# One decoder layer on one core: head pairs in prompt attention, another order of loads and of the MLP's steps, last product by token halves

## The reference

```
mods = silu(c) @ w_ada + b_ada                     # six vectors of 1024: shift, scale, gate, twice
h = rms_norm(x, norm_mix) * (1 + mods[1]) + mods[0]
q, k, v, u = split(h @ w_in, [512, 1024, 1536])    # w_in is 1024 x 2048
# prompt: causal softmax attention over blocks of 256 with a T5 bias (both blocks are in reach)
# samples: q . mean(k of each past block of 256), the top 3 of 16 blocks and the own tokens attend,
#          k and v come from pages of 128 rows through page_table
# pool:   trailing means of u over 2, 4, 8, 16, minus the token, times w_pool, times pool_scale
x = x + g1 * (concat(attn, pool) @ w_out)
h = rms_norm(x, norm_mlp) * (1 + sc2) + sh2
x = x + g2 * (square(relu(h @ w_up)) @ w_down)
y = rms_norm(x, norm_final)
```

## Time and profile before

| | |
|---|---|
| median of 3 runs | 983.2 us (982.89 to 991.43) |
| profiled execution | 986.67 us, its span 984.9 us |
| TensorE busy | 902.2 us, 92% |
| VectorE, ScalarE, GpSimd busy | 524.7, 231.2, 125.4 us |
| mean granted TensorE clock | 0.958 of 2.4 GHz |
| moved by DMA | 254.25 MB, 258 GB/s mean |

### The profile page before, as it was taken

How to read it: one execution, slowest core, us unless ns; L and a number is a source line. 1 busy time by engine, 2 the same in 40 slices (tenths; PEclk the granted TensorE clock), 3 DMA queues, 4 the chain that set the end, 5 groups by cost and what they waited for, 6 DMA issues and landing times.

```text
span 984.9 us, 16914 instructions
## 1 busy us (share of the span) xinstructions
PE 902.2 (92%) x6621; PEld 616.8 (63%) x6621; DVE 524.7 (53%) x968; ACT 231.2 (23%) x390; POOL 125.4 (13%) x134
## 2 busy tenths in 40 slices
PE   4699999999899887899899999899899799999896
PEld 3367775555676565666666666666666467675454
DVE  5533314787784766746756766667564232242224
ACT  3242204333220312220320320320220222213102
POOL 0006600000000000210210110110110111202100
PEclk8789999999999889899999999999999799999998
DMA  9902265888688586967977987887875957559992
GB/s 305 345 1 87 86 215 209 303 283 272 191 315 287 174 300 233 348 222 266 370 261 248 376 292 238 353 290 252 335 268 184 351 182 251 180 186 383 398 393 93
DMA packets 133282, 254.25 MB, mean 258 GB/s; under 512 B 10550, under 2 KB 61483, under 8 KB 125003
## 3 DMA queue, kind: packets, MB, share of 16 engines
q1 hardware_dynamic: 95571, 183.54, 53.0%
q10 hardware_dynamic: 36864, 67.13, 19.7%
q0 software_dynamic: 768, 2.51, 0.6%
HBM read 248.57 MB, written 4.75 MB: 257 GB/s over the span
## 4 chain that ended last, share of the span: by engine, by line
PE 70%; DVE 10%; DMA 8%; ACT 3%; issue 3%; ACTq 3%; SPq 1%; POOL 1%; DVEq 0%; POOLq 0%
PE PS L1523 68%; DVE KT L1120 4%; ACTq L849 3%; DMA VR<-in_cache_v_dram 2%; DMA VR<-in_w_up_dram 1%; DMA KR<-in_w_up_dram 1%; DMA KT<-in_w_up_dram 1%; ACT W_split L812 1%; PE PS L1692 1%; DMA W<-in_w_up_dram 1%; DMA X<-in_rel_bias_dram 1%; DMA KR<-in_cache_k_dram 1%; DVE smp L1239 1%; ACT smp L781 1%; PE PS L2098 0%
## 5 line engine op out<-in xcount | busy, mean ns | idle before, releaser
L1523 PE MATMUL PS<-H_split,W_split 128*128 128x512 f32 (+1 forms) x672 | 228.5, 401 | 2.0 <-DVE hT_split L1057 2.0
L1523 PE MATMUL PS<-gT_split,W_split 128*128 128x512 f32 x512 | 172.8, 402 | 3.0 <-POOL kT_split L681 3.0
L1120 DVE STREAM_TRANSPOSE KT<-KR 128x512 f32<-128x512 f32 x256 | 161.3, 680 | 18.7 <-DMA KR<-in_cache_k_dram 18.4
L1523 PEld LDWEIGHTS PS<-H_split,W_split 128*128 128x128 f32 x672 | 128.9, 195 | 50.0 <-issue 25.7
L1523 PE MATMUL PS<-hT_split,W_split 128*128 128x512 f32 (+1 forms) x336 | 131.5, 392 | 0.0
L1523 PEld LDWEIGHTS PS<-gT_split,W_split 128*128 128x128 f32 x512 | 96.1, 188 | 49.6 <-issue 18.7
L1270 DVE TENSOR_TENSOR W_split<-W,W_split 128x1024 fp32r<-128x1024 f32 x64 | 80.9, 1268 | 84.5 <-ACT W_split L812 84.5
L812 ACT ACTIVATE W_split<-W 128x1024 fp32r<-128x1024 f32 x64 | 67.2, 1052 | 230.1 <-DMA W<-in_w_up_dram 132.5
L1523 PE MATMUL PS<-KT,qcur 128*32 128x128 f32 (+1 forms) x2080 | 76.1, 289 | 29.0 <-DVE KT L1120 27.7
L1523 PE MATMUL PS<-kT_split,W_split 128*128 128x512 f32 x256 | 100.3, 392 | 0.0
L1309 DVE SCALAR_TENSOR_TENSOR xT<-PS,mods,xT 128x512 f32<-128x512 f32 x64 | 47.8, 749 | 80.6 <-PE PS L1523 80.6
(11 more groups left out here) (273 smaller groups left out, 963.2 us busy)
## 6 DMA issues: line engine op xcount, KB each, us to landing
KR<-in_cache_k_dram SPq DMA_DIRECT2D x256, 256.0 KB, 4.8
VR<-in_cache_v_dram ACTq DMA_DIRECT2D x256, 256.0 KB, 4.6
W<-in_w_up_dram SPq DMA_DIRECT2D x32, 512.0 KB, 6.7
W<-in_w_down_dram SPq DMA_DIRECT2D x32, 512.0 KB, 6.9
VR<-in_w_ada_dram SPq DMA_DIRECT2D x8, 1024.0 KB, 7.2
smp<-in_w_ada_dram SPq DMA_DIRECT2D x8, 1024.0 KB, 5.9
W<-in_w_in_dram SPq DMA_DIRECT2D x3, 2048.0 KB, 9.0
VR<-in_w_up_dram SPq DMA_DIRECT2D x3, 2048.0 KB, 10.6
```

Source lines behind the costliest of these rows:

```text
L1120: dve.transpose(ktb[:, t % 2, s, :], kring[:, t % 2, s, :]).then_inc(kt_ev, 1)
L1523: return pe.matmul(out, lhsT, rhs, start=start, stop=stop, **kw)
```

## The change

It is many edits at once; constants are `PAIRS = HP * TT` (16), `LAST = N_CH - 1`, `FINAL = (0, TT, 1, 2, 3)`, and TAIL_AT is gone. By place:

- Front: `load_ada(0)` is issued ahead of four small loads; TensorE's list goes modulation(0), state transposes, in_spread, modulation(1), (2), the bias matmuls (now in banks 6 and 0), modulation(3). VectorE evaluates the bias tables behind the last first_low. farb is negated, and the near bias gets it added at eviction (eight ScalarE copies of 256 columns for four of 512).
- Prompt attention goes by pairs of heads, q = (pair, tile).
- The half loads from j = 2 on are issued by ScalarE behind the eviction of pair j - 2.
- SyncE issues keys ahead of parts in every step; w_out for the samples in eight pieces, one a step at t = 66 to 73.
- The samples' output product is at t = 75, their MLP starts at t = 77; `sample_down(7)` is at 85.
- `values_ahead(t)` on ScalarE loads values t - LAG + 2, in step t behind some of its work; before, they were loaded first thing in step t + 1. TensorE weighs values ahead of `mlp(t, 0)` except at x == 3.
- VectorE turns keys ahead of weights_low at x == 1 and 3, and own_heads comes ahead of a weights_low at x == 2.
- `down` at x == 4 runs k = 0 to 2 of both tiles, then k = 3.
- The last chunk's down product goes by token halves, twice as many matmuls of 256 columns.

```diff
 # SyncE
+            for t in range(END + 1):          # first in the step, was behind the parts
+                if t + 2 < KT_ALL: ... load_keys(t + 2, k_ids)
+                if t == LAST_STEP:
+                    load_tail(0)
+                if t == LAST_STEP + 1:
+                    load_tail(1)
+                    load_tail(2)
+                if t >= LAST_STEP + 3:
+                    for n in (2 * (t - LAST_STEP - 3) + 2, 2 * (t - LAST_STEP - 3) + 3): ... load_tail(n)
...
-                    sp.dma_start(tail_slot(1), wout_d[:, :, 0:PIECE]).then_inc(tail_landed[1], 16)
-                    sp.wait_ge(qk, KT_ALL)
-                    sp.dma_start(tail_slot(2), wout_d[:, :, PIECE:D]).then_inc(tail_landed[2], 16)
+                if KT_ALL + 2 <= t < KT_ALL + 10:
+                    half, q = (t - KT_ALL - 2) // 4, (t - KT_ALL - 2) % 4
+                    sp.wait_ge(v_used, t - LAG)
+                    if half:
+                        sp.wait_ge(qk, KT_ALL)
+                    sp.dma_start(tail_slot(1 + half)[:, 2 * q:2 * q + 2, :],
+                                 wout_d[:, 2 * q:2 * q + 2, half * PIECE:(half + 1) * PIECE])\
+                      .then_inc(tail_landed[1 + half], 16)
 # ScalarE, attention
+            def exponentials(q):
+                n, s = (q % TT + 1) * P, 2 * (q % 2)
+                act.wait_ge(at_max, q + 1)
+                if q >= 2:
+                    act.wait_ge(at_pT, q - 1)
+                for e in range(2):
+                    act.activation(logits[:, s + e, 0:n], bank(e, P, n), ACT.Exp, bias=stat[:, s + e:s + e + 1],
+                                   accum_out=stat[:, 4 + s + e:5 + s + e]).then_inc(at_exp, 1)
+            def normalize(q):
+                act.wait_ge(at_rden, q + 1)
+                for e in range(2):
+                    act.activation(logits[:, s + e, 0:n], logits[:, s + e, 0:n], ACT.Copy,
+                                   scale=stat[:, 4 + s + e:5 + s + e]).then_inc(at_norm, 1)
+            for q in range(PAIRS):
+                if q + 1 < PAIRS:
+                    normalize(q + 1)
+                act.wait_ge(at_pT, q + 1)
+                if q:
+                    act.wait_ge(at_out, q)
+                for e in range(2):
+                    act.activation(pT[:, e, 0:n], bank(5 + e, P, n), ACT.Copy).then_inc(at_pT_ev, 1)
+                if q + 2 < PAIRS:
+                    act.wait_ge(ada_part, 4 + q + 1)
+                    act.dma_start(half_slot(q + 2), half_source(q + 2)).then_inc(half_landed[q % 2], 16)
+                if q + 2 < PAIRS:
+                    exponentials(q + 2)
+                if q > TT and q % TT == 1:
+                    attention_out(q // TT - 1)
 # ScalarE, MLP, x == 1 (x == 0, 5, 6, 7: values_ahead first; 2: behind relu; 3, 4: last)
                     relu(c, 0)
+                    values_ahead(t)
+                    hidden_high(c, 0)
                     if b < DB:
                         exps(b)
-                    hidden_high(c, 0)
                     weights_high(8 * c + 3 if c else 5)
 # VectorE, attention
+            def logits_in(q):
+                part = PS[:, 0:2, n - near:n]
+                link(dve.tensor_tensor(part, part, nearb[:, 2 * hp:2 * hp + 2, 2 * P - near:2 * P], ALU.add))
+                dve.tensor_reduce(stat[:, s:s + 2], PS[:, 0:2, 0:n], AX.X, ALU.max, negate=True).then_inc(at_max, 1)
+            def denominators(q):
+                dve.wait_ge(at_exp, 2 * q + 2)
+                dve.reciprocal(stat[:, 4 + s:6 + s], stat[:, 4 + s:6 + s]).then_inc(at_rden, 1)
+            for q in range(PAIRS):            # denominators(q+1), half_out(q), turn_keys, logits_in(q+2),
+                ...                           # half_modulation(q), turn_keys
 # VectorE, MLP, x == 1
+                    turn_unit(t + 1)
                     weights_low(8 * c + 3 if c else 5)
-                    turn_unit(t + 1)
 # TensorE, attention
+            def scores(q):
+                if q:
+                    pe.wait_ge(at_exp, 2 * q)
+                for e in range(2):
+                    r = slice(HD * e, HD * e + HD)
+                    last = mm(bank(e, P, (i + 1) * P), qT[r, hp, i * P:(i + 1) * P], kT[r, hp, 0:(i + 1) * P])
+                last.then_inc(at_scores, 1)
+            def weigh(q):
+                for kt in range(i + 1):
+                    for e in range(2):
+                        lo = HD * (2 * hp + e)
+                        last = mm(PS[HD * e:HD * e + HD, (4, 7)[hp % 2], i * P:(i + 1) * P], v_tok[:, kt, lo:lo + HD],
+                                  pT[:, e, kt * P:(kt + 1) * P], kt == 0, kt == i, skip_group_check=True)
+            for q in range(PAIRS):            # half_modulation(q), score_keys, scores(q+2), turn_prompt(q),
+                ...                           # weigh(q-1), fold_half(q)
 # TensorE, own values
-                    quarter(4, 0, probsT[0:NS, KEYS:], vS, False, True).then_inc(pv, 1)
+                    for q in range(QUADS):
+                        last = quarter(4, q, probsT[0:NS, KEYS:], vS[:, P * q:P * q + P], False, True, P, P * q)
 # TensorE, last chunk and end
+            def last_bank(j):
+                return bank((BANKS, (0, 1, 4, 7))[j // FT][j % 4], P, HALF, j // FT * HALF)
+                elif c == LAST and x == 4:
+                    for j in range(4):
+                        last_down(j, *((0, HP - 1), (HP - 1, HP))[half])
+                elif c == LAST:
+                    for j in range(2):
+                        last_down(4 * (x - 4) + 2 * half + j)
+                if t == END - 2:
+                    final_rows(0)             # between the halves; final_rows(1) behind the step
+                if t == END - 1:
+                    final_rows(2)             # between the halves; (3) and (4) behind the loop
```

More of the change, by code:

```diff
@@ L420, in softmax_of, with final_view, two @@
             return (t - 8) // 8
+        def final_view(p, n):
+            at = (2, 5)[p % 2]
+            return PS[0:n, at:at + 2, :]
+        def two(tile):
+            return tile.rearrange("p (a b) -> p a b", a=2)
+        def last_bank(j):
+            return bank((BANKS, (0, 1, 4, 7))[j // FT][j % 4], P, HALF, j // FT * HALF)
         @block.sync
@@ L1746, in _ @@
             scores(0)
-            scores(1)
             pe.wait_ge(bias_back, 16)
@@ L1972, in up, with down @@
                         ins.then_inc(up_ps, 1)
-            def down(c, m):
+            def down(c, m, first=0, end=HP):
                 if m >= 4:
                     pe.wait_ge(dn_ev, FT * c + m - 3)
-                for k in range(HP):
+                for k in range(first, end):
                     if m == 0:
```

605 lines of the change are left out of this document (309 added, 296 removed).

## The result

The changed kernel took 942.74 us (median of 4 runs, 940.84 to 947.47), the kernel before 984.3 us in the same set of runs; the ratio is 0.9564, 95% interval 0.9517 to 0.9610. Forecast were 936 us, range 922 to 954. The profiled execution took 941.84 us with a span of 940.0, against 984.9 before: 44.9 us less, where the sum said 47.7. One run of experiment 12 was in the chip's slower state and is left out of its median.

The account below looks back on a forecast made before the run. The prediction took TensorE, busy 92% with 70% of the chain, to bound the kernel, so only less TensorE work or fewer gaps could pay. Its eight terms summed to -47.7 us from 983.2, said as 936 us, range 922 to 954.

Parts of the forecast that it names:

- 1, front: Start to first projection product: bias matmuls fall where TensorE waits for DMA, projection begins at 48.4; -1.8 us.
- 2, attention: Prompt attention: a pair costs (4.1 + landing)/2, taken as 5.5 us, 93.7 in all; -2.3 us.
- rival (b): Prompt attention and own values: array parts don't overlap, 6.0 us a pair; 949 us in total, chance 0.09.
- (a): Prompt attention: half loads land late, 6.3 us a pair; 948 us in total, chance 0.17.
- 3, output stage: Output stage: keys issued ahead of parts end a late key unit, later parts cost nothing; -5.5 us.
- 4, chunks: MLP chunks 0 to 4: keys turned ahead of weight splits end TensorE's waits; chunk 0 -7.2 us, the others -14.2.
- 5, own values: Samples' own values: four parts of 128 columns run beside each other instead of 512-column matmuls; -5.3 us.
- 6, after the keys: Steps after the keys: w_out in pieces and earlier value loads end late values and half clock; -10.9 us.
- 7, tail: From 842.1 us to the end: stalls 4.5 us as before, end cut from 19.3 to 9; -5.5 us.
- 8, new waits: ScalarE's value loads wait for TensorE's weighing, and attention has half-clock spells; +5 us (0 to +15).
- (c): Seven chunks and stages: some 2.2 us of key wait returns in each as waiting for ScalarE; 951 us, chance 0.12.
- (d): Chunks with values: ScalarE's queue becomes the bound, 70 us over six chunks; 1006 us in total, chance 0.02.

Follow-up runs that it names:

- experiment 12: The changed kernel with three moves in its first half (bias products, add_sums at t = 16, value loads behind the same step's weighing): 959.09 us, ratio 0.9714.
- experiments 5 and 11: The changed kernel with w_out in two 2 MB loads (ratio 0.9604), and the changed kernel with the last down product by full width (945.3 us, ratio 0.9608).
- experiment 5: The changed kernel with w_out for the samples again as two 2 MB loads issued together: 942.4, 944.4, 953.3 and 954.2 us, ratio 0.9604.
- experiment 7: The changed kernel with the half loads of prompt attention issued by SyncE again: 943.88 us, ratio 0.9575.
- Experiment 6: The changed kernel with SyncE issuing keys behind the parts of the step again: 948.38 us, ratio 0.9614.
- experiment 1: The changed kernel with the samples' value weighing again between the two halves of the products in the MLP's steps: 966.45 us, ratio 0.9803.
- experiment 4: The changed kernel with the samples' own values again as one product of 512 columns: 948.64 us, ratio 0.9617.
- experiments 1 to 3: The changed kernel with one thing undone each: value weighing ahead of the products (966.45 us), VectorE's order at x == 1 and 3 (983.36), ScalarE's value-load place (954.22).
- Experiment 8: The changed kernel with half of the bytes of each load of the samples' MLP weights left out: 931.24 us, ratio 0.9460.

## Why the forecast held, point by point

**1, front: wrong, +1.5 for -1.8.** The step that failed: the bias matmuls would lie where TensorE waits for DMA. In the changed kernel:

```profile
33.55 1.92 PE L1580 MATMUL PS<-W,cT 128*32 128x512 f32 x16
37.76 1.69 PE L1580 MATMUL PS<-cst,sums 128*128 128x9 f32 x8 [2.29 <-DVE sums L1016]
39.38 4.94 PE L1580 MATMUL PS<-X 32*8 32x383 f32 x16
44.25 3.64 PE L1580 MATMUL PS<-KR,cT 128*32 128x512 f32 x16
```

TensorE is a chain of slow products and VectorE hand-overs by then, at 1.2 GHz in part; it reaches the fourth piece at 44.25 without a wait, 3.3 us after it did before. I had placed the work in a gap that belonged to the old order. It isn't the only step: in two of the traces (experiments 5 and 11) TensorE did come in time, at 41.7 and 41.9, and still began the projection at 50.0 and 50.2, since the product (3.64 us for the 2.8 forecast) and what follows ran at 1.2 GHz (granted clock 0.50 from 41.7 to 50.0 in experiment 5). In the twelve traces with this front the projection begins at 50.0 to 54.0, never near 48.4. (The terms of that sum give 48.2.)

**2, attention: right in size, its bound not shown: -6.3 for -2.3** (projection included; -4.7 without). Pairs 2 to 15 take 5.4 us each, 5.5 forecast. Of the 4.0 us beyond the forecast 2.4 lie in attention and are the chance of one trace: by the median of the other traces it is 2.9 us longer, 94.2 for the 93.7 forecast. Scores halved, where I took a quarter off: in the trace before, 512-column scores of two heads took 2.1 us, now 1.06. The weighing group of 16 products of 64 columns takes 1.02 us, 64 ns each for 128 before (the earlier trace rows has 8 of them in a group of 1.09); rival (b) is out. So is (a): its sign was there, gaps ahead of the half modulation in 6 of 16 pairs, at 0.65 us on average. The page of the Trainium skill that the forecast held against this move (Trainium Kernel Development and Optimization, Key Constraints: queues of SyncE and ScalarE share the 16 engines, only issue time is saved) agrees with the time of experiment 7 (943.9 for 942.7), and cuts both ways: the issuer is worth nothing that can be told in either direction. With it the forecast's formula for a pair, (4.1 + landing)/2, is in doubt: experiment 7 took the hand-over out of the 4.1, and a pair takes as long. TensorE waits for a load in six pairs only, all of slot VR.

**3, output stage: direction right, -1.7 for -5.5.** "The parts come later: nothing" was the step: the parts indeed cost nothing, the value pages did (2.4 us at 361, with slow clock behind it). The step of key unit 20 still takes 11.6 us, where the forecast had 8.2. Experiment 6 shows the exchange.

**4, chunks: the cause right, chunk 0 too high and the others too low.** Chunk 0 gave 3.6 of 7.9, since a wait of 2.8 for values (at 394, with a granted clock of 0.74 in that step) and one of 0.9 for smp fall into it. Chunks 1 to 3 gave 19.0 for 12.1: the waits for keys went as forecast, and a term is missing. The forecast named that TensorE weighs values ahead of the products and gave it no price. By experiment 1 it is 0.41 us in a plain step with keys. That is 1.2 us a chunk, or 1.6 if the third step, where the waits hide it, gains the same: 3.7 to 4.9 of the 6.9 us that chunks 1 to 3 gave beyond the forecast, and 6 to 8 in all. The rest stays open. A page of the Trainium skill states the rule that I left out (TensorEngine Tiling (Array Packing), Tiling Modes, Key Properties): a change of tiling mode, not merely of tile, drains TensorE. The traces fit it, with 0.2 us for each change between 32 and 128 columns.

**5, own values: right**, 0.35 us a group for 0.97, -5.0 of -5.3 (experiment 4).

**6, after the keys: right in sum.** From t = 56 to 75 it was -17.6; the forecast's terms give -16.9, and the joined order, which it did not count, pays in chunk 4 only (1.2 to 1.6), since without keys it saves no change. No value wait over 0.7 us is left. The pieces alone didn't remove it: with two big loads again the values were still in time (experiment 5).

**7, tail: wrong, +1.7 for -5.5.** The failed term is "stalls 4.5, as before". They were 12: 7.6 us around 857 (a wait of 4.40, then 1.2 GHz), 2.67 at 889, 1.09 at 906, and smaller ones. The two sides of it, VectorE and ScalarE:

```profile
855.54 1.22 DVE L1303 TENSOR_TENSOR W_split<-W,W_split 128x1024 fp32r<-128x1024 f32 x1 [10.58 <-ACT W_split L846]
856.68 0.68 DVE L1483 COPY scm<-PS 128x512 f32<-128x512 f32 x1
```
```profile
854.45 1.06 ACT L846 ACTIVATE W_split<-W 128x1024 fp32r<-128x1024 f32 x1 [10.48 <-DMA W<-in_w_up_dram]
```

Samples' weights and the last chunk's parts share a full DMA (share 1.05), a part lands at 854, and the sums' copy is queued behind its split. Three steps earlier, the samples' part shares its stretch with the parts; the 7.9 us of transfer against 4.7 of slack stood in my own sum, but I kept the old stalls instead of letting the difference show. The end, 9.6 us, was forecast at 9.0, though its terms as written add up to 9.65.

**8, new waits: not found.** ScalarE holds up no chunk: TensorE has 0.2 us of gaps in 64.8. Rivals (c) and (d) are out for the chunks; experiment 12 shows that (d)'s mechanism is real where ScalarE's own work stands behind such a load, in the output stage.

The total was right because errors cancelled. Chunks 1 to 3 gave 6.9 us more than forecast, the stretch behind them 0.7, attention with the projection 4.0, and 5.0 were charged for nothing: 16.6. Against them stand the front with 3.3, the output stage with 4.5, chunk 0 with 4.3 and the tail with 7.2: 19.3. That the total fell within 7 us owes something to luck. The parts aren't additive either: undone one by one, the three that are clear of noise (experiments 1 to 3) cost 76 us together, for 41.6 in all, since each was made with the others in place.

None of the versions that move all bytes is faster than the changed kernel. Experiment 8 says what the tail has to give, 11 us for 16 MB less. Moving them earlier needs slots that aren't free; that wasn't tried.

## What to carry to other kernels

Count the changes between products of different column widths in a step, and lay like beside like: two changes less gave 0.41 us of a 7.95 us step here, without a gap in the trace that would point there. When several queues are reordered together, price each order against the other engines' new places, not against the old trace; the dearest wait of the old order can grow (2.54 us to 4.61). Where a stretch has a DMA share of 1, moving a copy picked another wait, moving the issues cost 8.8 us, and only fewer bytes gave anything. And a stage of one trace is one sample: the same attention took 90.5 to 100.4 us.

## What was not expected of the hardware

A switch between 128x32 and 128x128 products costs 0.2 us without any gap showing in the trace (7.94 us with four against 7.54 with two, for equal work; 6.70 in both orders where both have two). Two heads' scores, in different 64-row parts of the array, overlap wholly: 1.06 us for two of 512 columns, 2.1 before. 1 MB loads issued 2 to 4 us sooner in a loaded stretch took 2.3 us longer to land (7.9 for 5.6 us, in one trace each).
